# Layernorm scaling in the mixer of a hybrid encoder block: from GpSimd passes to a second VectorE pass

## The reference

```
h  = LN0(concat(meta, x))
h1 = LN1(alpha*h + Mixer(h))       # projections, windowed attention, gated short convolution, W_o
h2 = LN2(alpha*h1 + HierMoE(h1))   # 32 experts, top 2
LN(x) = (x - mean) * rsqrt(var + eps) * g + b      # over the 1024 columns
```

## Time and profile before

| | |
|---|---|
| median of 3 runs | 4560.74 us (4558.6 to 4567.77) |
| profiled execution | 4558.93 us, span 4557.3 us |
| PE busy | 4181.0 us (92%) |
| PEld busy | 3531.3 us (77%) |
| DVE busy | 2486.4 us (55%) |
| ACT busy | 1640.8 us (36%) |
| POOL busy | 813.6 us (18%) |
| mean granted TensorE clock | 0.964 |

### The profile page before, as it was taken

The page is one execution under the profiler, slowest core; times in us unless marked ns, Lnnn a source line. Parts: engine busy times, 40 slices in busy tenths (PEclk is TensorE's granted clock), DMA queues, the critical chain, the costliest instruction groups (busy, mean ns, idle before and its releaser), DMA issues. The chain is left out here.

```text
span 4557.3 us, 68431 instructions
## 1 busy us (share of the span) xinstructions
PE 4181.0 (92%) x22196; PEld 3531.3 (77%) x22197; DVE 2486.4 (55%) x3696; ACT 1640.8 (36%) x2767; POOL 813.6 (18%) x741
## 2 busy tenths in 40 slices
PE   7999999999999999999999976999999999999700
PEld 7887887887887887888878865888888888888600
DVE  5555455456456446456555556554444555344388
ACT  2323323323323324224224222554444555344311
POOL 4022022022022112111211202000000000000176
PEclk9999999999999999999999988999999999999855
DMA  6233233333333333323323314774444565446387
GB/s 163 71 107 98 81 101 97 90 96 89 94 96 89 97 93 89 102 80 98 102 83 95 102 56 160 265 280 173 172 166 166 209 236 183 154 170 224 111 282 248
DMA packets 560688, 622.93 MB, mean 137 GB/s; under 512 B 90048, under 2 KB 412608, under 8 KB 560464
## 3 DMA queue, kind: packets, MB, share of 16 engines
q1 hardware_dynamic: 536992, 534.56, 36.1%
q0 software_dynamic: 23472, 85.47, 5.6%
HBM read 532.92 MB, written 87.03 MB: 136 GB/s over the span
## 5 line engine op out<-in xcount | busy, mean ns | idle before, releaser
L820 PE MATMUL bank<-hT_hi,w_hi 128*128 128x512 f32 x2176 | 864.9, 397 | 31.1 <-DVE w_lo L652 22.9
L652 DVE TENSOR_TENSOR w_lo<-raw,w_hi 128x1024 fp32r<-128x1024 f32 x400 | 598.0, 1495 | 484.6 <-ACT w_hi L511 483.4
L821 PE MATMUL bank<-hT_lo,w_hi 128*128 128x512 f32 x2176 | 850.6, 391 | 2.4 <-issue 2.4
L822 PE MATMUL bank<-hT_hi,w_lo 128*128 128x512 f32 x2176 | 849.0, 390 | 0.0
L1399 DVE TENSOR_TENSOR e_w_lo<-e_raw,e_w_hi 128x1024 fp32r<-128x1024 f32 x384 | 455.2, 1220 | 346.2 <-ACT e_w_hi L1357 343.2
L1454 PE MATMUL e_bank<-e_w_hi,e_xT_hi 128*128 128x256 f32 (+1 forms) x1968 | 627.0, 319 | 1.9 <-DVE e_xT_lo L1394 1.5
L1456 PE MATMUL e_bank<-e_w_hi,e_xT_lo 128*128 128x256 f32 (+1 forms) x1968 | 627.1, 319 | 0.0
L1455 PE MATMUL e_bank<-e_w_lo,e_xT_hi 128*128 128x256 f32 (+1 forms) x1968 | 626.9, 319 | 0.0
L820 PEld LDWEIGHTS bank<-hT_hi,w_hi 128*128 128x128 f32 x2176 | 408.9, 188 | 141.6 <-DVE w_lo L652 33.8
L822 PEld LDWEIGHTS bank<-hT_hi,w_lo 128*128 128x128 f32 x2176 | 408.9, 188 | 87.6
L821 PEld LDWEIGHTS bank<-hT_lo,w_hi 128*128 128x128 f32 x2176 | 409.2, 188 | 86.3 <-issue 5.3
(11 more groups left out here) (251 smaller groups left out, 6752.6 us busy)
## 6 DMA issues: line engine op xcount, KB each, us to landing
raw<-in_w_in_dram SPq DMA_DIRECT2D x251, 512.0 KB, 3.9
e_raw<-in_w_exp_gate_dram SPq DMA_DIRECT2D x128, 512.0 KB, 4.2
e_raw<-in_w_exp_up_dram SPq DMA_DIRECT2D x128, 512.0 KB, 9.0
e_raw<-in_w_exp_down_dram SPq DMA_DIRECT2D x128, 512.0 KB, 11.4
expert_rows<-e_y SPq DMA_DIRECT2D x82, 512.0 KB, 2.8
raw<-in_w_o_dram SPq DMA_DIRECT2D x64, 512.0 KB, 3.7
h_rows<-h_rows SPq DMA_DIRECT2D x36, 512.0 KB, 3.1
raw<-in_w_in_dram SPq DMA_DIRECT2D x64, 256.0 KB, 3.8
```

The source lines that it names most:

```text
L652: v.tensor_tensor(w_lo[:, s % 2, :], raw[:, s % RAW, :], w_hi[:, s % 2, :].bitcast(FP32), ALU.subtract).then_inc(lo_ready, 1)
L820: pe.matmul(out, hi, x_hi, start=first, stop=False)
L821: pe.matmul(out, hi, x_lo, start=False, stop=False)
L822: return pe.matmul(out, lo, x_hi, start=False, stop=last)
```

## The change

`scale` is taken from GpSimd, which keeps only `deviation` (lines 46 and 48). `normalize` on VectorE becomes two SCALAR_TENSOR_TENSOR passes over 128x1024, the second behind a semaphore of the first: (x - mean) * gain, then (that) * rstd + bias. The second raises `ln_done`. The place of `normalize` in the order of the strips stays.

```
-        ln_step, ln_moments, ln_rstd, ln_normed, ln_scaled, ln_done = (
+        ln_step, ln_moments, ln_rstd, ln_normed, ln_done = (
...
-                def scale(n, i1, rows, gain, shift):
-                    po.wait_ge(ln_normed, n + 1)
-                    po.tensor_tensor(rows[:, i1, :], rows[:, i1, :], gain[:, :], ALU.mult).then_inc(ln_scaled, 1)
-                    po.wait_ge(ln_scaled, n + 1)
-                    po.tensor_tensor(rows[:, i1, :], rows[:, i1, :], shift[:, :], ALU.add).then_inc(ln_done, 1)
-
                 with po.Fori(0, BLOCKS) as b:
                     deviation(b * LNS, 0)
                     for i1 in range(1, TILES):
                         deviation(b * LNS + i1, i1)
-                        scale(b * LNS + i1 - 1, i1 - 1, h, g1, b1)
-                    scale(b * LNS + TILES - 1, TILES - 1, h, g1, b1)
...
                     for i1 in range(TILES):
                         deviation(b * LNS + TILES + i1, i1)
-                        scale(b * LNS + TILES + i1, i1, xs, g0, b0)
...
                 def normalize(n, i1, rows):
                     v.wait_ge(ln_moments, n + 1)
                     v.wait_ge(ln_rstd, 2 * n + 2)
-                    v.tensor_scalar(rows[:, i1, :], rows[:, i1, :], moments[:, i1, 0:1], rstd[:, i1, 0:1],
-                                    ALU.subtract, ALU.mult).then_inc(ln_normed, 1)
+                    gain, shift = (g1, b1) if rows is h else (g0, b0)
+                    v.scalar_tensor_tensor(out=rows[:, i1, :], in0=rows[:, i1, :], scalar=moments[:, i1, 0:1],
+                                           in1=gain[:, :], op0=ALU.subtract, op1=ALU.mult).then_inc(ln_normed, 1)
+                    v.wait_ge(ln_normed, n + 1)
+                    v.scalar_tensor_tensor(out=rows[:, i1, :], in0=rows[:, i1, :], scalar=rstd[:, i1, 0:1],
+                                           in1=shift[:, :], op0=ALU.mult, op1=ALU.add).then_inc(ln_done, 1)
```

More of the change, by code:

```diff
@@ L416, in mixer @@
         hx_ready, hx_hi, hx_lo = sem("hx_ready"), sem("hx_hi"), sem("hx_lo")
-        ln_step, ln_moments, ln_rstd, ln_normed, ln_scaled, ln_done = (
-            sem("ln_step2"), sem("ln_moments2"), sem("ln_rstd2"), sem("ln_normed2"), sem("ln_scaled2"),
-            sem("ln_done2"))
+        ln_step, ln_moments, ln_rstd, ln_normed, ln_done = (
+            sem("ln_step2"), sem("ln_moments2"), sem("ln_rstd2"), sem("ln_normed2"), sem("ln_done2"))
         h_copied = sem("h_copied")
```

## The result

The changed kernel takes 4593.44 us in the median of 4 runs (4589.8 to 4594.1), beside 4560.54 us before (4558.6 to 4567.77): ratio 1.0068, 95% interval 1.0054 to 1.0082. Run again on another chip it took 4587.99 us beside 4567.89 us: 1.0052, 1.0038 to 1.0066. It is slower, by 33 and by 20 us (0.7% and 0.5%), and both intervals lie above 1; the forecast was 4583.0 us, in a range of 4573 to 4601. The profiled execution took 4594.1 us. One execution of the kernel before took 9031.2 us, twice the others, and is left out of every comparison.

The account below looks back on a forecast made before the run. PE, almost never idle in the block loop, was taken as the bound, through `w_lo`'s end. LN0's 42.9 us lost less LN1's 18.8 returned gave 24.1 us on 4558.93: 4583.0 us, 0.5% slower, range 4573 to 4601.

Parts of the forecast that it names:

- What bounds the kernel: Block loop: PE is busy 2611.35 of 2652.00 us, so only when `w_lo` is finished counts, not GpSimd time removed.
- LN0, 1.34 us in 32 places, 42.9 us: Ga strips, four per block: normalize ahead of `w_lo` makes PE stall 1.34 us, 32 times, 42.9 us lost.
- 0.56 us to spare: LN0's ga strips: `w_lo` can end 0.56 us later before PE is delayed.
- 2.52 us for two linked passes: LN0: normalize's follower on VectorE starts 2.52 us after normalize began, 1.79 us later than before.
- the restart's 0.11: PE after a wait: the step from first to second matmul is 0.34 us against 0.23, costing 0.11 us more.
- LN1, 18.8 us given back: Strips 5 and 7: contention with GpSimd ends, returning 1.48 and 0.87 us a block, 18.8 us in 8 blocks.
- over 1: Strip 5, LN1: `w_lo` is ready over 1 us before PE is due, so the stall goes wholly.
- The loop's head, taken as zero: Head of the block loop: no shift from 16 more VectorE instructions, bounded by 1 us a block either side, 8 us.
- rival 3: The loop's head moves with the longer body, up to 1 us a block: 4575 or 4591 us; chance 0.12 in all.
- Rival 1: Ga strips: the passes overlap or run faster, balance at about 0.91 us each, so not slower, 4553 us; chance 0.03.
- rival 2: LN1 gives back nothing, PE waits in strips 5 and 7 as before: 4602 us; chance 0.05.
- rival 4: LN0's stall is partly hidden for an unseen reason, its cost at half, 21.5 us: 4562 us; chance 0.04.

Follow-up runs that it names:

- ln0_alone: The kernel before with only LN0 changed to two VectorE passes, GpSimd keeping gain and bias of LN1: 4608.97 us, ratio 1.0097.
- ln1_alone: The kernel before with only LN1 changed to two VectorE passes, GpSimd keeping gain and bias of LN0: 4543.56 us, ratio 0.9962.
- no_scale: The kernel before without GpSimd's two wide passes, nothing put in their place, normalize still one TENSOR_SCALAR: 4544.3 us, ratio 0.9961.

## Why the prediction was right

- **What bounds the kernel**: that only `w_lo`'s end counts. Right: but for 1.2 us, the two traces of the mixer part nowhere but where `w_lo` moved, and 371 us of GpSimd's work were worth only the 18.5 us that they stood in the way.
- **LN0, 1.34 us in 32 places, 42.9 us**: measured 1.24 + 0.11, 43.2 in the changed kernel; in ln0_alone the last W_o matmul is 42.8 later. The 0.56 us to spare, the 2.52 us for two linked passes and the restart's 0.11 each came out within 0.01 to 0.02 us of what was put in. The pass is 1.28 us, as in L808, and not 1.42. The Trainium skill (VectorE: DVE Perf Modes, "The TRN2 errata", the formula (N+151)/0.96 ns under its cycle table) would make it 1.22 us, an estimate from a page whose formula is for `tensor_tensor`; the measured 1.276 to 1.287 us decides, and the sum by the page would have been 3.8 us lower.
- **LN1, 18.8 us given back**: 18.5 in strips 5 and 7 of the changed kernel and of ln1_alone, 18.4 in no_scale (their last W_o matmuls are 18.1 and 18.0 earlier, the loop's head included). Strip 5 has 1.22 us to spare, where "over 1" stood. L714 gave 0.86 a block for 0.87. The Trainium skill (SBUF — State Buffer, "Who interferes with whom") says that the loser of the shared pair waits for the other's whole instruction; the trace is in line with it: with GpSimd's wide ones gone, no L708 takes over 0.17 us.
- **The loop's head, taken as zero** (rival 3): 1.2 us over all 8 blocks. Single heads moved by up to 1.1 us in one step and most of it was met by steps the other way, so the bound of 8 us was never neared. (The "code loading" beside the earlier trace rows, which isn't part of the sum, is a guess: the trace has 11.0 us of ScalarE's idle time there, in 7 places, with issue alone as the cause.)
- **Rival 1** (passes at 0.91 us or less) fell with the 1.28 us, **rival 2** with ln1_alone, **rival 4** with the three points of stall against delay.
- **The number**: 24.1 us for the mixer, where the trace has 25.9. The first measured distance is 32.9, and the forecast time 10.4 us low. No term of the sum is off by more than 1.2 us; what it lacked was a term for how far two executions of the same combine stage lie apart: 8.6 us between the two of the changed kernel, 11 us between the extremes of all eleven profiles. So the mixer's 24.1 against 25.9 us is the mechanism, and how near the whole time came is luck in part. The range held it, but its terms add up to 4569 to 4603 and not to the 4573 to 4601 that were stated, and its width had been justified by the wrong things: "the runs' own spread" stood last in it, and was the largest part.

## What to carry to other kernels

Price a step on an engine with idle time by what is queued behind it on that engine and by how long before its deadline that is finished, at each place where the step stands. The same 2.5 us of VectorE cost 1.35 us ahead of `w_lo` in a ga strip, nothing behind it, and nothing in LN1, where it came with an end to contention that was worth more. Before taking out an engine's pass because it is long (3.3 us on GpSimd), look who waits for it: here nobody did in LN0, and all of the gain lay in LN1, so the change done for LN1 alone, or with LN0 behind `w_lo`, gains 17 to 20 us where the whole change loses 20 to 33.

## What the runs showed that I had not expected

A partial kernel that touches values ahead of a router can't be judged by its whole time: one tile more for the experts made 23 us, two made 33, more than the effect under study. And in the combine stage, where the DMA engines are busy 0.77 to 0.79 of the time, two executions of one kernel took 257.0 and 265.6 us with the same instructions.
